# VectorE's order in a step of the second block's attention: masks of a step before its Fourier units

## The chip, the cores and the metric

One core of a Trainium2 chip runs the whole program. The metric is the device time of one execution in microseconds; the figure for the kernel before is the median of three runs.

## The reference

Two layers of a first block (four kinds of attention) are followed by two layers of a second block, on 512 tokens of width 1024 in fp32. What the change touches is the second block's mixing stage:

```python
def second_block(x, ...):
    for l in range(DEPTH):
        h = rmsnorm(x, norm1[l])
        p = h @ w_in[l]                       # u | q | k | v
        y_f = fourier_mix(u, w_fourier[l], b_fourier[l])
        q, k = rope(rmsnorm(q, q_norm[l])), rope(rmsnorm(k, k_norm[l]))
        y_a = windowed_gqa(q, k, v, sink[l])
        mix = jnp.concatenate([rmsnorm(y_f, g_fourier_out[l]), rmsnorm(y_a, g_attn_out[l])], axis=-1)
        x = x + mix @ w_o[l]
        ...                                   # gated feed-forward with a 3-tap convolution

def fourier_mix(u, w_f, b_f):
    f = jnp.fft.fft2(u.astype(jnp.float32), axes=(1, 2), norm="ortho").real.astype(u.dtype)
    return f @ w_f + b_f
```

`windowed_gqa` is attention of 8 heads on blocks of 128 queries; each query sees keys at a distance of at most 128, and a sink term enters the softmax.

## The kernel before

Every engine has one instruction stream, written out by hand, and semaphores between them. Large products are made of three fp32r matmuls each (`r3`, recorded at L494): both operands are split into a rounded high part (ScalarE's copy) and a low part (VectorE's or POOL's subtraction). Weights come in chunks through two slots: SP loads, ScalarE rounds (L974), POOL subtracts (L480).

In the second block, the attention of a layer is 16 steps, each for a pair of heads (`par` 0 and 1) and one block of 128 queries; `qt` counts 0 to 3, and a step has 256 score columns where `qt` is 0 or 3, 384 where it is 1 or 2. Beside it runs the Fourier work, cut into units: `units_in_step` gives two per step in this block. Eight units make the rest of the u projection (its last six tiles, the first two in halves), eight the product A with the sequence DFT, four the tiles Pj, four the tiles Qj, then two are empty and four make y. They fill steps 0 to 14.

TensorE's step t (L531): scores of t (L542), after the exponentials of t-1; where `(t - 2) % 4 == 3` a spread of the inverse row sums over the partitions (`spread_heads`, L580); the product of probabilities and values for t-2 (L556); the transposes of the probabilities of t-1 (L566); the two units of t.

ScalarE's step t (L1007): the two units of t-1 (rounding of u at L1230 and of A at L1250, copies of Pj, rounding of the Fourier result at L1261), then the two exponentials of t (L1019), at `qt` 3 two sink terms (L1025), and the square of a finished output pair (L1277).

VectorE's step t (L1419): the two units of t-1, then masks and maxima of t (`mask_and_max`, L1465, with a read of the accumulator), then the row sums where due (L1479, L1480) and the copies of the transposed probabilities of t-1 (L1438), then work on finished pairs (`take_pair`, L1763, and sums of squares, L1658). VectorE's units, in `fourier` (L1716), are: the low part of a u tile (`u_lo`, L1710), that of an A tile (L1729), nothing for Pj, for each Qj the combination of Pj and Qj (L1739, L1740) and the low part of the result before (`f_lo`, L1755), later the sums of the squares of y (L1658).

Outputs of TensorE go to PSUM banks by a plan computed beforehand (`ring_plan`, L123). In this stage units and the spreads take banks 0 and 1 in turn, transposes banks 2 and 3, and a bank is taken again when the engine that reads its tile last has freed it: for u and A tiles VectorE's low part, for Pj ScalarE's copy, for Qj VectorE's combination, for y ScalarE. The spread of step 5 takes the bank of the first A tile of step 4. Before the first A tile TensorE waits for all u tiles of the second half to be freed, before the first Pj for the last four A tiles, before the first y for all four low parts of the Fourier result.

Of the kernel before, what the change touches and what calls it, by code (L numbers as in the profile page):

```python
# [117 lines left out]
def units_in_step(block, t):  # L118

    return 3 if block == 1 and t < 6 else 2  # L120
# [112 lines left out]
def build(nc, dram, out):  # L233
# [3 lines left out]
    with ctx:  # L237
# [101 lines left out]
        def S(name):  # L339
            if name not in sems:  # L340
                sems[name] = ctx.enter_context(nc.semaphore(name))
            return sems[name]
# [20 lines left out]
        def bank(name):  # L363
            return banks[ring[name][1]]

        def wait_full(eng, name, i=None, per=0):

            v = ring[name][0] + 1
            eng.wait_ge(S("ring_full"), v if i is None else i * per + v)

        def freed(name):
            return S(f"ring_freed{ring[name][1]}")
# [8 lines left out]
        def per_row(tile, it):  # L381

            c = 4 * it["par"] + it["qt"]
            return tile[:, it["o"] % 2, c:c + 1]
# [26 lines left out]
        block = ctx.enter_context(nc.Block())  # L411
# [940 lines left out]
        def _(dve):  # L1352
# [66 lines left out]
            def attention(pairs, l, block, finish, between, scale_gate=None):  # L1419
                N = len(pairs)  # L1420
                for t in range(N + 5):
                    if t >= 1:
                        for _ in range(units_in_step(block, t - 1)):
                            next(between, None)
                    if t < N:
                        for it in pairs[t]:
                            dve.wait_ge(S("scores_ready"), it["n"] + 1)
                            mask_and_max(it, l).then_inc(S("max_ready"), 1)
                    if 1 <= t <= N:
                        pair = pairs[t - 1]  # L1430
                        if pair[0]["qt"] == TT - 1:
                            row_sums(pair)
                        for it in pair:
                            n, w = it["n"], it["nb"] * P
                            wait_full(dve, ("T", n))
                            if t >= 2:
                                dve.wait_ge(S("pv_done"), n - 1)
                            v.tensor_copy(probs_t[:, it["par"], 0:w], bank(("T", n))[:, 0:w]).then_inc(freed(("T", n)), 1)  # L1438
                    if scale_gate and t >= 2 and (t - 2) % TT == TT - 1:
                        scale_gate(pairs[t - 2][1])  # L1440
                    if t >= 3 and (t - 3) % TT == TT - 1:
                        finish(pairs[t - 3][1], 0)
                    if t >= 4 and (t - 4) % TT == TT - 1:
                        finish(pairs[t - 4][1], 1)
                for _ in between:
                    pass

            def mask_and_max(it, l):

                w, nb, b, h = it["nb"] * P, it["nb"], it["branch"], it["h"]  # L1450
                s, top = s_bank[it["par"]][:, 0:w], per_row(neg_max, it)
                blocks = s.rearrange("p (b c) -> p b c", c=P)
                m0 = it["k0"] - it["qt"] + 1
                if b == "M":
                    return v.tensor_reduce(top, s, AX.X, ALU.max, negate=True)  # L1455
                if b == "A":
                    return v.tensor_tensor_reduce(out=s, in0=s, in1=bias_r[:, h, w - 1::-1], scale=-1.0, scalar=BIG,  # L1457
                                                  op0=ALU.add, op1=ALU.min, accum_out=top)
                if b == "B":
                    return v.tensor_tensor_reduce(out=blocks[:, ::-1, :], in0=blocks[:, ::-1, :], in1=masks[:, 1:1 + nb, :], scale=-1.0,  # L1460
                                                  scalar=BIG, op0=ALU.add, op1=ALU.min, accum_out=top)
                if b == "C":
                    return v.tensor_tensor_reduce(out=blocks, in0=blocks, in1=masks[:, m0:m0 + nb, :], scale=-1.0,
                                                  scalar=neg_sink[:, l, h:h + 1], op0=ALU.add, op1=ALU.min, accum_out=top)
                return v.tensor_tensor_reduce(out=blocks, in0=blocks, in1=masks[:, 5 + m0:5 + m0 + nb, :],  # L1465
                                              scale=head_inv[:, it["pair"], it["qt"], it["par"]:it["par"] + 1],
                                              scalar=neg_sink[:, l, 4 + h:5 + h], op0=ALU.add, op1=ALU.min, accum_out=top)
# [3 lines left out]
            def row_sums(pair):  # L1471

                it = pair[1]
                sums = row_sum[:, it["o"] % 2, :]
                dve.wait_ge(S("exp_done"), it["n"] + 1)
                if it["sink"]:
                    sinks[0] += 2
                    dve.wait_ge(S("sink_exp"), sinks[0])
                    step(v.tensor_tensor(sums, sums, sink_exp[:, :], ALU.add))  # L1479
                v.reciprocal(row_inv[:, it["o"] % 2, :], sums).then_inc(S("inv_ready"), 1)  # L1480
# [27 lines left out]
            for l in range(DEPTH):  # L1508
# [63 lines left out]
                def scale_gate(it):  # L1572
                    n, tile, name = it["o"] % 8, it["tile"], ("bc", it["o"])
                    if n in (0, 2):
                        for t in range(2):
                            wait_taken(dve, ("w", l, f"{'am'[n // 2]}g{t}"))
                    if n == 4:
                        dve.wait_ge(S("gates_ready"), l + 1)
                        wait_taken(dve, ("w", l, "cg1"))
                    if n >= 6:  # L1580
                        wait_taken(dve, ("w", l, f"bg{n - 6}"))
                    wait_full(dve, name)
                    v.tensor_tensor(g[:, tile, :], bank(name)[:, :], g[:, tile, :], ALU.mult).then_inc(freed(name), 1)

                def gate_pair(it, part):
# [5 lines left out]
                    elif n == 7:  # L1591
                        out_lo(l, n)

                attention(PAIRS[l], l, 1, gate_pair, later_projections(), scale_gate)

                def centred_pair(k):
# [46 lines left out]
            for l in range(DEPTH):  # L1643
# [114 lines left out]
                def take_pair(it, part):  # L1758
# [5 lines left out]
                    elif k >= 1:  # L1764
                        sum_squares("ya", ya_squares, k)

                attention(PAIRS[DEPTH + l], l, 2, take_pair, fourier())
                wait_taken(dve, ("mix_ms", l))
                v.reciprocal(rtok[:, :], stat[:, :]).then_inc(S("mix_inv"), 1)
# [213 lines left out]
```

## Time and profile before

| | us |
|---|---|
| median of 3 runs | 1852.99 (1846.31 to 1853.43) |
| profiled execution | 1850.35 |
| its span | 1848.4 |
| TensorE busy (matmul) | 1750.2 |
| VectorE busy | 776.8 |
| ScalarE busy | 701.2 |
| POOL busy | 692.2 |

The profile records one execution: for each instruction its start, duration, line and engine (PE is TensorE, DVE VectorE, ACT ScalarE). Ends of matmuls are modelled, so durations in a row of matmuls overlap; starts are used below. In a timeline row "x4" means that four records were merged, and the duration then runs from the first start to the last end; what stands in brackets is the idle time of the engine before the instruction and what ended it. The windows give the busy time of each engine in a stretch and the clock that TensorE was granted, 1.00 being 2.4 GHz.

### The profile page before, as it was taken

What the parts mean: (1) busy time and instruction counts of PE and PEld (TensorE: products, weight loads), DVE (VectorE), ACT (ScalarE), POOL (GpSimd) and SP (SyncE); (2) the same over time, 40 slices, a digit from 0 to 9 for tenths busy, and PEclk for the clock granted to TensorE, in tenths of its full rate; (3) what the DMA queues carried; (4) which work ended last, traced back from release to release, by engine and by line L of the source; (5) the groups of instructions that cost most, each with busy time, mean ns of one, the idle gap of its engine ahead of it and who ended that gap; (6) DMA issues with size and microseconds to landing.
All of it is one profiled execution on the core that took longest, in us unless ns stands there. A gap on an engine that the chain in (4) does not pass through costs nothing.

```text
span 1848.4 us, 24688 instructions
## 1 busy us (share of the span) xinstructions
PE 1750.2 (95%) x9084; PEld 1379.2 (75%) x9084; DVE 776.8 (42%) x1470; ACT 701.2 (38%) x1136; POOL 692.2 (37%) x553
## 2 busy tenths in 40 slices
PE   6998999899899989989999999999997999999999
PEld 5775568787566767867788888877785878888887
DVE  7126464402655264554455115522455345502441
ACT  4444441524445053444343223433355334312331
POOL 3423116442310642325344344345231634434433
PEclk9999989899998979999999999999999999999999
DMA  6211103221110211112222223122211222232222
GB/s 254 92 69 47 47 24 118 89 91 70 47 47 24 103 40 53 70 47 69 91 91 79 101 98 107 67 98 88 70 50 44 91 91 91 74 108 92 102 74 95
DMA packets 24895, 148.02 MB, mean 80 GB/s; under 512 B 3184, under 2 KB 3568, under 8 KB 10736
## 3 DMA queue, kind: packets, MB, share of 16 engines
q1 hardware_dynamic: 22128, 140.13, 21.7%
q10 hardware_dynamic: 2688, 6.82, 1.0%
q8 instruction: 52, 0.85, 0.2%
q14 instruction: 27, 0.22, 0.0%
HBM read 144.84 MB, written 2.10 MB: 79 GB/s over the span
## 4 chain that ended last, share of the span: by engine, by line
PE 50%; issue 31%; POOL 11%; DVE 3%; ACT 3%; DMA 1%; POOLq 0%; ACTq 0%; DVEq 0%
PE ring L494 38%; POOL w_lo L480 11%; PE scores L542 3%; PE ring L566 2%; PE outs L556 2%; PE ring L580 1%; PE ring L637 1%; DMA xt<-in_x 1%; ACT probs L1019 1%; PE ring L874 1%; DVE g L1664 1%; PE ring L610 1%; ACT w_hi L974 1%; POOL w_hi L470 1%; DVE mix_l L1669 0%
## 5 line engine op out<-in xcount | busy, mean ns | idle before, releaser
L480 POOL TENSOR_TENSOR w_lo<-w_stage,w_hi 128x258 fp32r<-128x258 f32 (+5 forms) x517 | 670.7, 1330 | 1116.6 <-ACT w_hi L974 691.1
L494 PE MATMUL ring<-xh,w_lo 128*128 128x512 f32 x1296 | 522.3, 403 | 36.0 <-POOL w_lo L480 14.5
L494 PE MATMUL ring<-xh,w_hi 128*128 128x512 f32 x1296 | 515.4, 398 | 0.0
L494 PE MATMUL ring<-xl,w_hi 128*128 128x512 f32 x1296 | 515.1, 397 | 0.0
L494 PEld LDWEIGHTS ring<-xh,w_lo 128*128 128x128 f32 x1296 | 246.9, 191 | 100.3 <-issue 15.5
L494 PEld LDWEIGHTS ring<-xh,w_hi 128*128 128x128 f32 x1296 | 246.7, 190 | 56.5
L494 PEld LDWEIGHTS ring<-xl,w_hi 128*128 128x128 f32 x1296 | 247.3, 191 | 53.6
L1305 ACT ACTIVATE w_hi<-w_stage 128x2048 fp32r<-128x2048 f32 (+2 forms) x72 | 120.5, 1673 | 158.7 <-PE ring L494 158.7
L1315 ACT ACTIVATE g<-ring,convw 128x512 f32<-128x512 f32 x88 | 68.2, 779 | 261.3 <-DVE ring L1800 261.3
L974 ACT ACTIVATE w_hi<-w_stage 128x2064 fp32r<-128x2064 f32 (+2 forms) x77 | 123.0, 1607 | 88.2 <-PE ring L494 87.9
L1019 ACT ACTIVATE probs<-scores,neg_max 128x256 f32<-128x256 f32 (+2 forms) x192 | 96.1, 503 | 131.4 <-DVE neg_max L1455 28.2
L494 PE MATMUL ring<-act_l,w_hi 128*128 128x512 f32 x352 | 139.7, 397 | 0.0
L494 PE MATMUL ring<-act_h,w_lo 128*128 128x512 f32 x352 | 139.1, 395 | 0.0
L494 PE MATMUL ring<-act_h,w_hi 128*128 128x512 f32 x352 | 138.5, 394 | 0.0
L1800 DVE TENSOR_TENSOR ring<-ring,tmp 128x512 f32<-128x512 f32 x88 | 61.2, 699 | 183.0 <-PE ring L494 173.1
L1782 DVE TENSOR_TENSOR xt<-xt,ring 128x512 f32<-128x512 f32 x48 | 33.0, 687 | 248.2 <-PE ring L494 248.2
L1438 DVE COPY probs_t<-ring 128x256 f32<-128x256 f32 (+2 forms) x192 | 79.8, 455 | 35.8 <-PE ring L566 34.7
L494 PEld LDWEIGHTS ring<-act_h,w_lo 128*128 128x128 f32 x352 | 66.0, 188 | 17.2 <-DVE act_l L1813 0.7
L494 PEld LDWEIGHTS ring<-act_h,w_hi 128*128 128x128 f32 x352 | 66.0, 188 | 16.0
L494 PEld LDWEIGHTS ring<-act_l,w_hi 128*128 128x128 f32 x352 | 66.0, 188 | 15.6
L1457 DVE CUSTOM_DVE_ANT_0 scores<-scores,bias_r 128x128 f32<-128x128 f32 (+3 forms) x32 | 15.1, 514 | 135.9 <-PE scores L542 135.9
L566 PE MATMUL ring<-ident,probs 128*128 128x128 f32 x440 | 72.2, 294 | 0.0
(266 smaller groups left out, 2319.8 us busy)
## 6 DMA issues: line engine op xcount, KB each, us to landing
w_stage<-in_mixed SPq DMA_DIRECT2D x64, 1032.0 KB, 4.8
w_stage<-in_up SPq DMA_DIRECT2D x44, 1024.0 KB, 4.9
w_stage<-in_down SPq DMA_DIRECT2D x16, 768.0 KB, 4.3
w_stage<-in_down SPq DMA_DIRECT2D x16, 640.0 KB, 3.8
xt<-in_x ACTq DMA_DIRECT2D x4, 512.0 KB, 11.5
out_t<-xt ACTq DMA_DIRECT2D x8, 256.0 KB, 2.0
mem_f<-in_mem SPq DMA_DIRECT2D x1, 1024.0 KB, 9.8
bias_r<-in_relb SPq DMA_DIRECT2D x1, 1024.0 KB, 11.1
```

Of the source, the lines that this page charges most:

```text
L480: ins = nc.gpsimd.tensor_tensor(w_lo[:, slot, cols], w_stage[:, slot, cols], w_hi[:, slot, cols].bitcast(F32), ALU.subtract)
L494: ins = nc.tensor.matmul(o, lhs, rhs, start=start, stop=stop, skip_group_check=True)
L542: nc.tensor.matmul(s_bank[it["par"]][:, 0:it["nb"] * P], q_of(it), k_of(it, l), start=True, stop=True, skip_group_check=True).then_inc(S(" ...
L556: ins = nc.tensor.matmul(o_bank[it["o"] % 2][lo:lo + 64, it["qt"] * P:it["qt"] * P + P], v_of(it, l, j), probs_t[:, it["par"], j * P:j * P ...
L566: ins = nc.tensor.transpose(o[:, j * P:j * P + P], probs[:, it["n"] % 3, j * P:j * P + P], ident[:, :])
L974: ins = A(w_hi[:, c % 2, first:last], w_stage[:, c % 2, first:last], ACT.Copy)
L1019: A(probs[:, n % 3, 0:w], s_bank[it["par"]][:, 0:w], ACT.Exp, bias=per_row(neg_max, it), scale=1.0 if it["branch"] == "M" else -1.0, accum ...
L1305: A(w_hi[:, c % 2, 0:width], w_stage[:, c % 2, 0:width], ACT.Copy).then_inc(S("w_hi_done"), 1)
L1315: A(g[:, 4 * s + 2 + v, :], bank((kind, l, f0 + first + s))[:, :], ACT.Identity, bias=convw[:, l, taps, 4 * v + 3:4 * v + 4], scale=convw[ ...
L1438: v.tensor_copy(probs_t[:, it["par"], 0:w], bank(("T", n))[:, 0:w]).then_inc(freed(("T", n)), 1)
L1782: v.tensor_tensor(xt[:, k, :], xt[:, k, :], bank(name)[:, :], ALU.add).then_inc(freed(name), 1)
L1800: v.tensor_tensor(bank(name)[:, :], bank(name)[:, :], tmp[:, 0, :], ALU.mult).then_inc(S("normed"), 1)
```

## The change

In VectorE's attention loop the units of t-1 keep their place for block 1. For block 2 they are issued after the masks and maxima of step t instead of before them; they still come before the row sums and copies of the step. The instructions themselves, their number and their semaphores are the same, and so are the streams of the other engines.

```diff
--- before.py
+++ after.py
@@ -1419,13 +1419,16 @@
             def attention(pairs, l, block, finish, between, scale_gate=None):
                 N = len(pairs)
                 for t in range(N + 5):
-                    if t >= 1:
+                    if t >= 1 and block == 1:
                         for _ in range(units_in_step(block, t - 1)):
                             next(between, None)
                     if t < N:
                         for it in pairs[t]:
                             dve.wait_ge(S("scores_ready"), it["n"] + 1)
                             mask_and_max(it, l).then_inc(S("max_ready"), 1)
+                    if t >= 1 and block == 2:
+                        for _ in range(units_in_step(block, t - 1)):
+                            next(between, None)
                     if 1 <= t <= N:
                         pair = pairs[t - 1]
                         if pair[0]["qt"] == TT - 1:
```

## Rows read from the trace of the kernel before

**Rows 1.** The page's span, then windows of both stages: busy us (count) by engine, clock.

```profile
span 1848.4 us, 24688 instructions
...
725.00:822.00 97.00, 90.46 (x744) 74.93 (x746) 51.06 (x141) 48.47 (x115) 34.64 (x48) 0.98 0.19 67
1317.00:1413.00 96.00, 89.08 (x752) 74.03 (x752) 51.32 (x141) 49.41 (x116) 34.67 (x48) 1.00 0.20 67
```

**Rows 2.** Timeline, first layer, step 6: start, duration, instruction, idle before it.

```profile
759.89 0.92 PE L542 MATMUL scores<-k,q 64*128 64x384 f32 x4
...
760.84 0.69 DVE L1465 CUSTOM_DVE_ANT_0 scores<-scores,masks,neg_sink 128x384 f32<-128x384 f32 x1
...
761.96 0.36 PE L494 MATMUL ring<-w_hi,u_l 128*128 128x258 f32 x1
...
762.04 1.02 DVE L1438 COPY probs_t<-ring 128x384 f32<-128x384 f32 x2
```

**Rows 3.** Timeline, first layer, steps 4 and 5.

```profile
748.95 0.70 PE L542 MATMUL scores<-k,q 64*128 64x256 f32 x4
...
750.80 0.36 PE L494 MATMUL ring<-w_hi,u_l 128*128 128x258 f32 x1
...
754.15 0.92 PE L542 MATMUL scores<-k,q 64*128 64x384 f32 x4 [0.23 <-ACT probs L1019]
...
754.40 0.76 DVE L1729 TENSOR_TENSOR a_l<-ring,a_h 128x258 fp32r<-128x258 f32 x2 [2.35 <-ACT a_h L1250]
...
754.99 1.09 PE L580 MATMUL ring<-ident,row_inv 128*64 128x128 f32 x16
...
755.10 0.69 DVE L1465 CUSTOM_DVE_ANT_0 scores<-scores,masks,neg_sink 128x384 f32<-128x384 f32 x1
```

**Rows 4.** Timeline, first layer, step 11 to the start of step 13.

```profile
784.65 0.42 DVE L1739 TENSOR_TENSOR sq<-pj,ring 128x257 f32<-128x257 f32 x1
...
785.92 0.70 PE L542 MATMUL scores<-k,q 64*128 64x256 f32 x4
...
788.38 0.47 ACT L1019 ACTIVATE probs<-scores,neg_max 128x256 f32<-128x256 f32 x1 [0.80 <-DVE neg_max L1465]
...
790.33 1.31 DVE L1658 TENSOR_TENSOR tmp<-tmp 128x512 f32<-128x512 f32 x1 [0.65 <-ACT tmp L1277]
...
791.57 0.41 DVE L1739 TENSOR_TENSOR sq<-pj,ring 128x257 f32<-128x257 f32 x1
...
794.03 0.63 ACT L1261 ACTIVATE f_h<-sq 128x512 fp32r<-128x512 f32 x1 [1.00 <-DVEq L1742]
...
795.47 0.47 ACT L1019 ACTIVATE probs<-scores,neg_max 128x256 f32<-128x256 f32 x1 [0.81 <-DVE neg_max L1465]
...
796.56 1.65 PE L542 MATMUL scores<-k,q 64*128 64x384 f32 x4 [3.39 <-ACT probs L1019]
```

**Rows 5.** Timeline, first layer, step 15 to the last spread.

```profile
815.85 0.70 PE L542 MATMUL scores<-k,q 64*128 64x256 f32 x4
...
816.58 0.55 DVE L1465 CUSTOM_DVE_ANT_0 scores<-scores,masks,neg_sink 128x256 f32<-128x256 f32 x1 [1.35 <-PE scores L542]
...
817.05 0.55 DVE L1465 CUSTOM_DVE_ANT_0 scores<-scores,masks,neg_sink 128x256 f32<-128x256 f32 x1
...
817.87 1.02 DVE L1438 COPY probs_t<-ring 128x384 f32<-128x384 f32 x2 [0.21 <-PE ring L566]
...
819.04 0.88 PE L556 MATMUL outs<-probs_t,v 128*64 128x128 f32 x12 [0.88 <-DVE probs_t L1438]
...
819.42 0.69 DVE L1658 TENSOR_TENSOR tmp<-tmp 128x512 f32<-128x512 f32 x1 [0.53 <-ACT tmp L1277]
...
821.08 1.09 PE L580 MATMUL ring<-ident,row_inv 128*64 128x128 f32 x16 [0.58 <-DVE row_inv L1480]
```

**Rows 6.** Windows from the scores of step 13, first and second layer, as in rows 1.

```profile
796.60:799.60 3.00, 3.00 (x18) 1.92 (x20) 2.04 (x6) 0.00 (x0) 0.00 (x0) 0.50 0.03 5
1388.60:1391.60 3.00, 2.91 (x33) 2.19 (x34) 2.40 (x7) 0.04 (x1) 0.00 (x0) 1.00 0.04 11
```

## The prediction

> **What bounds the kernel now.** I read the span and the windows of the two second-block attention stages first, because only these stages are touched [rows 1]. TensorE is busy 90.5 of 97 us in the first layer and 89.1 of 96 in the second, at full clock but for one stretch, while VectorE works 51 us. So TensorE's instruction stream sets the end, and a stage gets longer by exactly the time that TensorE newly waits, shorter only by a wait that it loses. 6.5 and 6.9 us of waits are there to be lost, in all. Then I read the timelines of single steps, always from the start of the scores of step t, which I write S(t), and asked two things: how late TensorE needs something that VectorE gives, and how late VectorE gives it once the pair of masks stands in front.
>
> In one step TensorE issues scores(t), at steps 5, 9, 13 the spread of the inverse sums, the probabilities-times-values of t-2, the transposes of t-1, then two units of Fourier work. VectorE, before, did the two units of t-1, masks of t, copies of t-1. The first unit's low part was mostly done while TensorE still worked on the second unit, the second one's in the gap between S(t) and the moment at which the masks could start. The masks could not start much earlier: on an idle VectorE they start 0.73 us after S(t) with 256 columns [rows 5], and in step 6, with the low part just finished, 0.95 us after S(t) with 384 columns [rows 2]. Step 5 has the same 0.95 [rows 3], though its low parts ended elsewhere, so I take it for the floor of a wide step; nothing is then gained there, and in a narrow step 0.1 to 0.3 us that nobody waits for. Were the floor 0.73 in wide steps too, (a) and (b) below would each be 0.2 less.
>
> **The change part by part.** No instruction is added or removed, no DMA is moved; POOL's and SP's queues see only later releases. What moves is a pair of masks ahead of two units. A pair holds VectorE 1.20 us at 384 columns (760.84 to 762.04, [rows 2]) and 0.93 at 256 (twice 816.58 to 817.05, [rows 5]). The new wait for scores(t) now stands in front of the units of t-1, so these are queued behind S(t) + 2.15 us (384) or S(t) + 1.66 us (256). Who waits for them is TensorE, through the two ring banks 0 and 1 that all units share.
>
> (a) Steps 3 to 8, the unit's bank. In step 6 the first unit needs the bank of the first A tile of step 5. It starts at S + 2.07 (759.89 to 761.96, [rows 2]); the low part will be done at 0.95 + 1.20 + 0.43 = 2.58, 0.43 us being one low part, of which two take 0.76 [rows 3]. Stall 0.5. In step 4 the first A tile needs all u tiles split, thus both low parts: 0.73 + 0.93 + 0.76 = 2.42, against 1.85 (748.95 to 750.80, [rows 3]): stall 0.6. Step 8 has the same pattern (the P tiles need both last A tiles): 0.6. Steps 3 and 7 need one low part at 0.73 + 0.93 + 0.43 = 2.09, against the 2.07 of the six-transpose pattern: 0. Steps 1 and 2 need nothing of the step itself. Together 1.7.
>
> (b) Step 5. The spread of the inverse sums comes right behind the scores, and its bank is that of the first A tile of step 4. Before, the two low parts ran at 754.40, before the spread at 754.99, S + 0.84 [rows 3]. The mask already started at 755.10, S + 0.95, so it gains nothing, and the bank comes free at 0.95 + 1.20 + 0.4 = 2.55. Stall 1.7. At steps 9 and 13 the spread's bank is not waited for: its last holders are a P tile, freed by ScalarE, and the third Q tile, freed a step before.
>
> (c) Steps 11 to 13, the Fourier pairs. I call ft the pair of VectorE instructions that combines a P and a Q tile. ScalarE rounds two ft results before it takes the exponentials of the step, and this order is unchanged. Before, ft(0) ran at 784.65, ahead of S(11) = 785.92. Now it starts at 785.92 + 1.66 = 787.58; ft(1) follows after some 0.85 (two instructions of 0.42 [rows 4]), ScalarE can round it at 789.3 and reach its exponentials at 789.9, not at 788.38: 1.5 later. (TensorE's third Q tile would meanwhile wait 0.4 for its bank; this is inside the sum below, not added.) The square that ScalarE makes behind them, and VectorE's sum of it, which began at 790.33, come at 791.85. That sum took 1.31 us while POOL was splitting weights, against 0.69 of the same line later [rows 4, 5]; so it ends at 792.5 to 793.1 instead of 791.57, and the masks of step 12 start there, since S(12) is past. From that point the old path to the exponentials was 795.47 - 791.57 = 3.90; the new one is 0.93 of masks, 2.46 to the second rounding (791.57 to 794.03), and 0.6 of rounding: 3.99. So scores(13), which already waited 3.39 us for these exponentials [rows 4], start 1.0 to 1.6 later. I take 1.3. The masks are off this chain in name only: what ends last is the exponential behind two roundings, and they now wait for the masks.
>
> The Trainium skill (GPSIMD Engine Reference, Specifications) says that GpSimd shares its SBUF interfaces with VectorE and collides with VectorE instructions that have two SBUF inputs. The 1.31 against 0.69 us agrees with that; one pair of rows is little, and POOL may be done by then, so I let the price be open between the two.
>
> (d) Steps 15 to 17. Two sums of y squares were done before the masks of step 15, in idle time; now they stand between masks and copies. The masks end at 817.51; two sums at 0.62 follow; the copies that began at 817.87 begin at 818.75, and TensorE's product, which already waited for them until 819.04, starts 0.9 later. What ends last is VectorE's chain: the sum at 819.42 moves to some 819.8, and the last spread at 821.08 by the same 0.4 [rows 5]. Price 0.4, and 0.9 if the chain doesn't catch up.
>
> Step 13's own rest (the last low part behind the masks) is hidden: it ends at S(13) + 0.95 + 1.20 + 0.7 = 2.85, and before the y tiles TensorE has the spread (at 0.84, for 1.09 [rows 3]) and some 1.0 of product and transposes (1.15 with six transposes, [rows 2]), together 2.9; at most 0.1.
>
> **Sum.** 1.7 + 1.7 + 1.3 + 0.4 = 5.1 us per layer. The second layer repeats the pattern to some hundredths, so 10.2 in all. Behind the stage come projections bound by TensorE that hide nothing. The profiled execution took 1850.35 us (span 1848.4 and 1.95 around it), 2.64 below the median of 1852.99; the sum gives 1860.6 against the one and 1863.2 against the other. I take 1862. Bounds per layer: (a) 0.8 to 2.2 (each stall 0.2 us less or 0.1 more), (b) 1.4 to 1.9, (c) 0.9 to 1.7, (d) 0.2 to 0.9; no part can be a gain of more than 0.1, as nothing that TensorE waits for comes sooner. 3.3 to 6.7, thus 6.6 to 13.4 in all.
>
> **Rivals.** First, the other sign: the early masks bring the exponentials of step 12 forward and shorten TensorE's wait of 3.39 us at S(13). If ScalarE met its exponentials first, masks (0.93) and one low part (0.7) would leave that chain: 1.6 per layer, 1847; it decides as soon as the banks of (a) and (b) turn out free in time. Against it speaks ScalarE's order, with both roundings ahead. 7 in 100, with everything from 1846 to 1852.
>
> Second, the clock. After the 3.39 us wait of the first layer the granted clock was 0.50 over 3 us, the 1.2 GHz level, and the scores took 1.65 us; in the second layer, after an equal wait, it stayed at 1.00 [rows 4, 6]. At half clock 3 us of work cost 1.5 more. New idle of 1.7 us in step 5 and a longer one at S(13) could bring one to three such stretches: 1.5 to 4.5 us, 1863.5 to 1866.5. That layer kept full clock through all its waits, 6.9 us of them [rows 1]. 22 in 100. The Trainium skill (TensorE: Matmul & The Clock Gate, HAM oscillation) warns that idling between groups of matmuls brings the low clock back again and again; the first layer agrees, the second doesn't. By it alone each layer would lose once more, 1865.
>
> Third, only the chains cost: the bank stalls of (a) and (b) are mostly absorbed, because the profile's ends are modelled and low parts release earlier than I read. Then (c) + (d) remain, 1.7 per layer: 1855.5. 14 in 100.
>
> **How the numbers follow.** The forecast, 1858 to 1865 about 1862, has 57 in 100. The range 1855 to 1868 leaves out the first rival and the far end of the second. Half a per cent, about what a measurement of this kernel can tell from no change, is 9.3 us: 1862.3 against the median. The forecast's sum lies little above it, so it gives two thirds of its weight to slower; the second rival nearly all; the third none. Slower 0.60, same 0.37, faster 0.03.
>
> **What would show it.** In the changed profile: TensorE's L580 of step 5 starts 2.5 us after its scores, with a wait of 1.7 put to the low part at L1729, in both layers; first units of steps 4 and 8 at S + 2.4 and of step 6 at S + 2.6; masks at S + 0.95 or S + 0.73 in every step, no sooner; the wait of scores(13) for L1019 at 4 us or more; the copies of step 15 about 1.2 us after its masks end. Both stages longer by 5, all others as before. I am wrong if L580 of step 5 still starts at S + 0.84, if the exponentials of step 12 come less than 3.9 us after S(12), or if the granted clock falls in step 5.

## The result and the profile after

| | before | after |
|---|---|---|
| median of the runs, us | 1851.49 (1846.31 to 1853.43, 4 runs) | 1867.37 (1864.29 to 1871.61, 4 runs) |
| profiled execution, its span | 1850.35, 1848.4 | 1864.29, 1862.5 |
| TensorE busy | 1750.2 | 1757.9 |
| VectorE busy | 776.8 | 774.6 |

The ratio of the runs is 1.0092, 95% interval 1.0061 to 1.0123: the changed kernel is 11 to 23 us slower, some 16 by the medians. The forecast of 1862 had the sign and the places; it had about 9 to 10 us where 16 to 17 came. Carried over to the 1852.99 us that the prediction started from, the ratio gives 1870, beyond the upper end of its range, 1868.

In the changed kernel the lines of VectorE's code move by three: the masks are at L1468, the low parts of u and A at L1713 and L1732, the combination at L1742 and L1743, `f_lo` at L1758, the copies at L1441, the sums of squares at L1661.

**Steps 4, 5 and 6** (answers to [rows 2, 3]). Timeline of the changed kernel, first layer; the columns are start, duration, instruction, and idle time before it with what ended it.

```profile
749.57 0.70 PE L542 MATMUL scores<-k,q 64*128 64x256 f32 x4
...
751.24 0.87 DVE L1713 SCALAR_TENSOR_TENSOR u_l<-ring,rtok,u_h 128x256 fp32r<-128x256 f32 x2
...
752.37 0.36 PE L494 MATMUL ring<-w_hi,u_l 128*128 128x258 f32 x1 [0.70 <-DVE u_l L1713]
...
755.71 0.92 PE L542 MATMUL scores<-k,q 64*128 64x384 f32 x4 [0.23 <-ACT probs L1019]
...
756.66 0.69 DVE L1468 CUSTOM_DVE_ANT_0 scores<-scores,masks,neg_sink 128x384 f32<-128x384 f32 x1 [3.47 <-PE scores L542]
...
757.86 0.76 DVE L1732 TENSOR_TENSOR a_l<-ring,a_h 128x258 fp32r<-128x258 f32 x2
...
758.43 1.09 PE L580 MATMUL ring<-ident,row_inv 128*64 128x128 f32 x16 [1.80 <-DVE a_l L1732]
...
763.35 0.92 PE L542 MATMUL scores<-k,q 64*128 64x384 f32 x4
...
765.97 0.39 PE L494 MATMUL ring<-w_hi,u_l 128*128 128x258 f32 x1 [0.32 <-DVE a_l L1732]
```

The mask of step 5 starts 0.95 us after the scores, as before. VectorE had been idle 3.47 us by then, and through the last of it two A tiles, rounded by 756.20, waited for their low parts. The low parts follow at 757.86, and the spread, which came 0.84 us after the scores, now comes 2.72 after them. The A tile of step 4 comes 2.80 us after its scores instead of 1.85, the unit of step 6 2.62 instead of 2.07. In step 8 (scores at 774.26) the first P tile waits for two low parts of A, which end at 776.68 (the view shows 0.75 us for the pair), and comes 2.78 us after its scores:

```profile
775.93 0.75 DVE L1732 TENSOR_TENSOR a_l<-ring,a_h 128x258 fp32r<-128x258 f32 x2
...
777.04 0.36 PE L494 MATMUL ring<-a_h,w_lo 128*128 128x258 f32 x1 [0.69 <-DVE a_l L1732]
```

**Step 11 to the start of step 13** (answers to [rows 4]), same kernel and layer.

```profile
791.00 0.70 PE L542 MATMUL scores<-k,q 64*128 64x256 f32 x4
...
792.67 0.42 DVE L1742 TENSOR_TENSOR sq<-pj,ring 128x257 f32<-128x257 f32 x1
...
794.55 0.98 DVE L1758 TENSOR_TENSOR f_l<-sq,f_h 128x512 fp32r<-128x512 f32 x1 [0.16 <-DVE sq L1743]
...
795.02 0.46 ACT L1019 ACTIVATE probs<-scores,neg_max 128x256 f32<-128x256 f32 x1
...
796.95 0.69 DVE L1661 TENSOR_TENSOR tmp<-tmp 128x512 f32<-128x512 f32 x1 [0.36 <-ACT tmp L1277]
...
797.56 0.55 DVE L1468 CUSTOM_DVE_ANT_0 scores<-scores,masks,neg_sink 128x256 f32<-128x256 f32 x1
...
801.50 0.46 ACT L1019 ACTIVATE probs<-scores,neg_max 128x256 f32<-128x256 f32 x1
802.55 1.65 PE L542 MATMUL scores<-k,q 64*128 64x384 f32 x4 [3.95 <-ACT probs L1019]
```

From the masks of step 12 to its exponentials are 3.94 us; the old path was 3.90. Scores(13) start 11.55 after scores(11), before it was 10.64.

**The end of the stage** (answers to [rows 5]).

```profile
822.43 0.70 PE L542 MATMUL scores<-k,q 64*128 64x256 f32 x4
...
823.17 0.55 DVE L1468 CUSTOM_DVE_ANT_0 scores<-scores,masks,neg_sink 128x256 f32<-128x256 f32 x1 [4.81 <-PE scores L542]
...
825.50 1.01 DVE L1441 COPY probs_t<-ring 128x384 f32<-128x384 f32 x2
...
826.66 0.88 PE L556 MATMUL outs<-probs_t,v 128*64 128x128 f32 x12 [1.92 <-DVE probs_t L1441]
...
828.37 1.98 PE L580 MATMUL ring<-ident,row_inv 128*64 128x128 f32 x16
```

Two sums of squares now stand between masks and copies; TensorE's product waits 1.92 us instead of 0.88. And the spread takes 1.98 us instead of 1.09, at half clock.

**The clock** (answers to [rows 1, 6]). Windows of the changed kernel: the numbers at the end of a line are granted clock, DMA share and GB/s.

```profile
725.00:841.00 116.00, 101.31 (x786) 83.47 (x787) 55.62 (x150) 54.12 (x123) 34.10 (x48) 0.93 0.16 56
1322.00:1438.00 116.00, 101.37 (x788) 83.44 (x789) 55.63 (x151) 54.65 (x123) 34.07 (x48) 0.94 0.16 56
...
828.00:831.00 3.00, 3.00 (x27) 2.46 (x25) 0.88 (x3) 0.60 (x1) 0.00 (x0) 0.50 0.00 0
834.00:845.00 11.00, 9.26 (x33) 7.54 (x33) 7.97 (x14) 4.67 (x8) 0.00 (x0) 0.53 0.00 0
1397.00:1405.00 8.00, 5.78 (x35) 4.29 (x36) 4.78 (x14) 1.55 (x6) 0.00 (x0) 0.57 0.10 42
```

The same 116 us of the kernel before, from its own start of the stage:

```profile
725.00:841.00 116.00, 104.90 (x815) 85.69 (x816) 63.51 (x161) 58.70 (x130) 36.44 (x51) 0.97 0.16 56
1317.00:1433.00 116.00, 104.55 (x821) 85.61 (x822) 63.77 (x161) 60.06 (x130) 37.90 (x53) 0.99 0.16 56
```

At a clock of 0.93 and 0.94 instead of 0.97 and 0.99 the changed kernel spent about 30 us of the two stretches at the 1.2 GHz level, before about 10. The 3.4 us behind scores(13) in one layer have become some 7 in both (0.57 over the 8 us from 1397 is 6.9 us at half clock), and the 3.4 us behind the last spreads of each layer have become two pieces, in the first layer one of them some 10 us long.

**Length of each step**, from the starts of its scores to those of the next, worked out from the timelines (us):

| from the scores of step | before, 1st layer | after | before, 2nd layer | after |
|---|---|---|---|---|
| 3 | 7.94 | 8.10 | 7.70 | 7.86 |
| 4 | 5.20 | 6.14 | 5.21 | 6.13 |
| 5 | 5.74 | 7.64 | 5.76 | 7.64 |
| 6 | 5.11 | 5.71 | 5.14 | 5.72 |
| 7 | 5.12 | 5.20 | 5.12 | 5.23 |
| 8 | 4.90 | 5.84 | 4.90 | 5.82 |
| 9, 10 together | 10.90 | 10.90 | 10.89 | 10.89 |
| 11 | 5.15 | 5.51 | 5.13 | 5.55 |
| 12 | 5.49 | 6.04 | 5.52 | 6.01 |
| 13 | 11.45 | 12.04 | 9.87 | 12.34 |
| 14 | 7.84 | 7.84 | 7.82 | 7.82 |
| 15 to the last spread L580 | 5.23 | 5.94 | 5.24 | 5.66 |
| on to the spread L619 | 5.55 | 6.75 | 5.55 | 6.75 |
| on to the output projection | 4.46 | 4.93 | 4.48 | 4.92 |

The rows "on to" are TensorE's work behind the last step: it spreads the inverse norms (L619) and begins the output projection. From scores(0) to the output projection the two layers take 114.27 and 114.00 us instead of 105.75 and 103.98, 18.5 us more. The span grew by 14.1 only: outside the stages the profiled execution of before had more half clock than that of after (of the shift, 3 us came back in front of the second layer's attention and 1 us in each feed-forward), which no experiment here addresses. The timed runs had 16.

### The profile page after: what moved, and what is told of

Read it like the earlier page. It is cut to its first block, busy times and chain, and to the rows that moved or that the text cites. A ratio compares the mean times of both kernels' runs of the same rounds, so it can differ in the third digit from the quotient of the medians.

```text
span 1862.5 us, 24682 instructions
## 1 busy us (share of the span) xinstructions
PE 1757.9 (94%) x9084; PEld 1385.4 (74%) x9084; DVE 774.6 (42%) x1470; ACT 701.2 (38%) x1136; POOL 690.7 (37%) x553
## 4 chain that ended last, share of the span: by engine, by line
PE 49%; issue 31%; POOL 11%; DVE 4%; ACT 3%; DMA 1%; POOLq 0%; ACTq 0%; DVEq 0%
PE ring L494 38%; POOL w_lo L480 11%; PE scores L542 3%; PE ring L566 2%; PE outs L556 2%; PE ring L580 1%; PE ring L637 1%; ACT probs L1019 1%; DMA xt<-in_x 1%; PE ring L874 1%; DVE scores L1468 1%; DVE g L1667 1%; PE ring L610 1%; ACT w_hi L974 1%; POOL w_hi L470 1%
## 5 line engine op out<-in xcount | busy, mean ns | idle before, releaser
L1441 DVE COPY probs_t<-ring 128x256 f32<-128x256 f32 (+2 forms) x192 | 80.1, 456 | 38.3 <-PE ring L566 37.2
L494 PEld LDWEIGHTS ring<-act_l,w_hi 128*128 128x128 f32 x352 | 66.0, 188 | 15.6
L1468 DVE CUSTOM_DVE_ANT_0 scores<-scores,masks,neg_sink 128x256 f32<-128x256 f32 (+1 forms) x64 | 36.8, 617 | 97.0 <-PE scores L542 97.0
```

Of the source, the lines that this page charges most:

```text
L494: ins = nc.tensor.matmul(o, lhs, rhs, start=start, stop=stop, skip_group_check=True)
```

## The experiments

Ratios and differences are against the kernel before, run on the same chip and at the same time as the experiment. The changed kernel was timed apart from them, so a comparison of an experiment with it goes over two measurements.

**Step 5 alone.** VectorE's order of the change, for one step of sixteen:

```diff
-                    if t >= 1:
+                    late = t >= 1 and block == 2 and (t == 5)
+                    if t >= 1 and not late:
                         for _ in range(units_in_step(block, t - 1)):
                             next(between, None)
                     ...                                    # masks and maxima of t
+                    if late:
+                        for _ in range(units_in_step(block, t - 1)):
+                            next(between, None)
```

> Masks first in step 5 of the second block alone. My theory (the banks 0 and 1 that units and spreads share): the spread of step 5 starts 2.7 us after its scores instead of 0.84, with a wait of 1.8 put to the low part of A, in both layers; every other step keeps its length; +1.9 us a layer, +3.8 in all, the clock rows as before. If instead the change costs by its chains in steps 11 to 17 alone (rival), this kernel takes the time of before, within 1 us.

Measured: 1.0032 (1.0018 to 1.0047), 1854.31 against 1849.10 us. Step 5 takes 7.62 us instead of 5.74 in the first layer, every other step up to the twelfth keeps its length, and the wait is put to the low part. Timeline of this kernel in the second layer:

```profile
1349.87 0.92 PE L542 MATMUL scores<-k,q 64*128 64x384 f32 x4 [0.23 <-ACT probs L1019]
1352.58 1.48 PE L580 MATMUL ring<-ident,row_inv 128*64 128x128 f32 x16 [1.80 <-DVE a_l L1733]
1353.78 1.13 PE L556 MATMUL outs<-probs_t,v 128*64 128x128 f32 x8
```

The window right behind it, read as those above:

```profile
1355.00:1357.00 2.00, 2.00 (x12) 2.00 (x13) 0.85 (x2) 1.16 (x3) 0.00 (x0) 0.61 0.62 153
```

The wait is the same 1.80 us, but here the clock fell right behind it, and step 5 took 9.21 instead of 5.76. In the first layer it did not fall. So the bank's wait is shown. A second cost beside it, which the expectation had left out, shows in one layer of the trace, and this execution (1861.03 us) was the second slowest of the kernel's twelve. The times alone don't show it: 3.8 us were expected, some 6 came, and the interval reaches from 3.3 to 8.7.

**Steps 1 to 10 alone** (the condition is `t <= 10`).

> Masks first in steps 1 to 10 alone. Theory: steps 3 to 8 grow by 0.2, 0.9, 1.9, 0.6, 0.1 and 0.9 us as in the changed kernel, 4.6 a layer and 9.2 in all; the wait at scores(13) stays 3.4 us and the low clock behind it as before. If the low clock of the changed kernel comes from the many new waits of steps 3 to 8, it shows here too, with another 2 to 5 us.

Measured: 1.0065 (1.0049 to 1.0080), 12 us. The steps have the lengths of the changed kernel to 0.05 us (steps 4 to 8 of the first layer: 6.14, 7.64, 5.70, 5.22, 5.85), 4.6 us a layer, and steps 11 and 12 those of before. The 9.2 us of stalls lie just inside the interval (9.1 to 14.8). In the trace step 13 takes 11.50 us in both layers where the second layer of before had 9.87, behind an unchanged wait; but with the old order it took 11.26 to 12.28 in the other layers too (first layer of the kernel before, both layers with step 5 alone and with steps 15 and 16 alone), so this is no cost of the change. The way from the last spread to the next is 5.55 us in both layers, as before. Where the other 3 us are, if they are real, is open.

**From step 11 on alone** (`t >= 11`).

> Masks first from step 11 on alone. Theory: steps 11 and 12 grow by 0.4 and 0.5 us, the end of the stage by 0.5: 1.4 a layer, 2.8 in all, and on top what a longer wait at scores(13) (3.9 instead of 3.4 us) brings in half clock, 0 to 2.5 us a layer. If half clock belongs to steps 3 to 8, the sum stays at 2.8.

Measured: 1.0035 (1.0016 to 1.0054), 6.5 us. Steps 11 and 12 take 5.54 and 6.02 in the first layer, 5.56 and 5.99 in the second; from scores(15) to the last spread 5.66 and 5.90. That is the 1.4 us a layer. The trace shows half clock beside it: step 13 at 12.55 and 11.45, the way to the next spread at 6.13 and 6.76 instead of 5.55. The interval is 3.0 to 10 us, so that the 2.8 of stalls is just outside it. The longer way to the next spread, which steps 1 to 10 alone don't have, belongs to this half of the change. The two ratios add to 1.0100, the whole change had 1.0092.

**The masks between the two units.**

```diff
-                    if t >= 1:
-                        for _ in range(units_in_step(block, t - 1)):
-                            next(between, None)
+                    units = units_in_step(block, t - 1) if t >= 1 else 0
+                    for _ in range(units if block == 1 else min(units, 1)):
+                        next(between, None)
                     ...                                    # masks and maxima of t
+                    for _ in range(0 if block == 1 else units - 1):
+                        next(between, None)
```

> The masks of a step come between its two Fourier units: the first unit's low part ahead of them, the second's behind. Theory: whoever waits for the first unit only (the spread of step 5, the first unit of steps 3, 6, 7 and the third Q tile) waits no more; steps 4 and 8, where TensorE needs both, keep 0.5 to 0.7 us each, and one postponed result remains in the chains of steps 11 to 17: 1.2 us a layer in steps 3 to 8, against 4.6 of the changed kernel; 2.5 to 5 us in all above before. If what costs is that the masks hold VectorE at all, and not which bank is behind them, the time is that of the changed kernel, +14.

Measured: 1.0020 (1.0005 to 1.0035), 3.7 us where 2.5 to 5 were expected. Timeline of this kernel, steps 4 and 5 of the first layer:

```profile
751.46 0.36 PE L494 MATMUL ring<-w_hi,u_l 128*128 128x258 f32 x1 [0.31 <-DVE u_l L1712]
...
755.06 0.43 DVE L1731 TENSOR_TENSOR a_l<-ring,a_h 128x258 fp32r<-128x258 f32 x1 [2.78 <-ACT a_h L1250]
755.65 1.09 PE L580 MATMUL ring<-ident,row_inv 128*64 128x128 f32 x16
755.75 0.69 DVE L1467 CUSTOM_DVE_ANT_0 scores<-scores,masks,neg_sink 128x384 f32<-128x384 f32 x1 [0.27 <-PE scores L542]
```

With the first low part ahead of the masks, the spread is back at 0.85 us after its scores (754.80), steps 3, 5, 6, 7 and 11 have their old lengths, and only steps 4 and 8, where TensorE needs both low parts, keep 0.54 and 0.61. The masks start when they did. What costs is which bank stands behind the masks, not the time that they hold VectorE.

**The changed kernel, with work in TensorE's wait.** At the end of step 12 TensorE multiplies the identity by itself into the bank that the next spread overwrites; the results are used by nothing.

```diff
                     for _ in range(units_in_step(block, t)):
                         next(between, None)
+                    if block == 2 and t == 12:
+                        name = ("bc", pairs[11][0]["o"])
+                        pe.wait_ge(freed(name), ring[name][2])
+                        for _ in range(22):
+                            nc.tensor.matmul(bank(name)[:, 0:P], ident[:, :], ident[:, :], start=True, stop=True, skip_group_check=True)
```

> The changed kernel, with 22 more matmuls (identity by identity, 128 columns, into the ring bank that the next spread will overwrite) at the end of TensorE's step 12, so that TensorE works in most of its wait at scores(13). They take about 2.3 us of a wait of 3.9 and delay nothing. Theory: if half clock follows from that wait, steps 13 to 14 take 9.9 us in both layers instead of 12.0 and 12.3, and the kernel gains 2 to 5 us on the changed one (1863 to 1865 beside 1867). If the clock falls by a phase of its own, the length of step 13 is unchanged or random and the time that of the changed kernel.

Measured: 1864.39 us, 1.0076 (1.0058 to 1.0094). My size was off: one such matmul takes 0.235 us, 22 take 5.2 and not 2.3, so scores(13) came 1.8 us late.

```profile
798.89 5.18 PE L574 MATMUL ring<-ident 128*128 128x128 f32 x44 [0.66 <-DVE sq L1748]
804.00 0.92 PE L542 MATMUL scores<-k,q 64*128 64x384 f32 x4
```

But the scores took 0.92 us and not 1.65, and step 13 took 10.09 us in both layers, where the changed kernel had 12.04 and 12.34.

**The kernel before with 26 of them.**

> The kernel before with 26 such matmuls in the wait of 3.4 us at scores(13). Theory: half clock behind this wait disappears where it came (step 13 at 9.9 us instead of 11.5 in the first layer); 0 to 3 us less than before. Rival (a phase of its own): no change.

Measured: 1.0020 (1.0008 to 1.0032). Too long again: step 12 took 7.83 instead of 5.5 us. Step 13 took 9.88 in both layers. Inconclusive as a time; both fillings were repeated with 12.

**The changed kernel with 12.**

> The changed kernel with 12 matmuls in its wait at scores(13) instead of 22: one takes 0.235 us, 12 some 2.8 us of the 3.2 in which their bank is free, so that step 12 keeps its 6.0 us. Theory (a wait costs its length and then half clock): step 13 at 9.9 to 10.1 us in both layers instead of 12.0 and 12.3, 4 us less than the changed kernel, about 1863, and 12 to 13 us above before, which is the sum of the stalls alone. If the clock is no part of the cost, no difference from the changed kernel, 17 above before.

Measured: 1862.67 us, 1.0059 (1.0043 to 1.0075), 12.0 us above before.

```profile
801.94 2.94 PE L574 MATMUL ring<-ident 128*128 128x128 f32 x24 [0.65 <-DVE sq L1748]
...
805.21 0.92 PE L542 MATMUL scores<-k,q 64*128 64x384 f32 x4 [0.32 <-ACT probs L1024]
```

Scores(13) come where they came, with 0.32 us of wait left instead of 3.95, and step 13 takes 10.08 and 10.09 us. This kernel computes the same and does more, and is 4.7 us below the changed kernel's median; the intervals of the two ratios overlap, so this difference by itself is not shown. The expected 1863 and 12 to 13 us came; the way to the spread L619 stayed at 6.75 in both layers, so half clock at the end of the stage is still in it.

**The kernel before with 12.**

> The kernel before with 12 such matmuls. Theory: step 12 keeps 5.5 us, step 13 takes 9.9 in both layers; 1 to 3 us less than the kernel before in the mean, as it has half clock there in at least one layer. Rival: no difference.

Measured: 0.9978 (0.9966 to 0.9989), 3.6 us faster than before. Step 12 keeps 5.49 and 5.51, step 13 takes 9.88 in both layers.

```profile
796.33 0.92 PE L542 MATMUL scores<-k,q 64*128 64x384 f32 x4 [0.72 <-ACT probs L1024]
```

This kernel and the one before it were timed together, and they differ by nothing but the change: 1862.67 against 1847.04 us, 15.6 us, with full clock in step 13 of both layers of both. That is about what the change cost without the matmuls. The matmuls take 3.6 us from the order of before and 4.7 from the changed one, nearly the same: half clock behind scores(13) is paid in both orders.

**Low parts behind the masks, everything else ahead.** In steps 11 and 12 of the kernel before, only the last `f_lo` of the step goes behind the masks.

```diff
                     ...                                    # masks and maxima of t
+                    while postponed:
+                        low_part[0](postponed.pop(0))
                     ...                                    # in the units of the Qj
-                        if j >= 1:
-                            f_lo(j - 1)
+                        if j == 2:
+                            f_lo(1)
+                        if j % 2 == 1:
+                            postponed.append(j - 1)
                         yield
```

> The kernel before, its units ahead of the masks, but in steps 11 and 12 the last low part (L1755) goes behind the masks of the step: the chain to the exponentials loses it, and nothing is put into it. Theory of the chain (steps 11 to 13: what ends last is the exponential behind masks and roundings): masks of step 11 start 0.7 us sooner and those of step 12 1.4 us sooner, scores(13) wait 2.0 us instead of 3.4; 2.8 us less in both layers, and perhaps 1.5 to 3 us more if the clock stays up. If ScalarE's order sets the wait alone, nothing changes.

Measured: 1.0004 (0.9992 to 1.0017), no difference. The chain did what was expected in size:

```profile
789.03 1.08 DVE L1761 TENSOR_TENSOR f_l<-sq,f_h 128x512 fp32r<-128x512 f32 x1
...
796.51 0.92 PE L542 MATMUL scores<-k,q 64*128 64x384 f32 x4 [2.31 <-ACT probs L1019]
```

Step 12 takes 4.40 and 4.42 us instead of 5.5, 1.1 us less in each layer (1.4 expected; a low part beside POOL took 1.08 us here, not 0.69). The clock took it back in the profiled execution: step 13 is 11.49 and 12.55 us, the way from the last spread on 6.36 and 5.79.

**The same with 10 matmuls in the wait.**

> The one before this, with 10 matmuls more in the wait of 2 us at scores(13). Theory: as before this, with full clock in step 13 of both layers for certain: 3 to 6 us less than the kernel before.

Measured: 0.9976 (0.9965 to 0.9988), 3.3 us faster than before. Step 12 keeps 4.4 us and step 13 takes 9.87 in both layers. Timed together with the kernel above, from which it differs by the 10 matmuls alone, it takes 1846.44 us against 1851.09.

**Steps 15 and 16 alone** (`t in (15, 16)`).

> Masks first in steps 15 and 16 alone. My prediction had 0.4 us a layer. Theory from the trace of the changed kernel: from scores(15) to the last spread 5.7 us instead of 5.2, 0.9 in all; and if the longer wait before the product of step 16 (1.9 instead of 0.9 us) brings half clock, the way from the last spread to the next takes 6.4 to 6.8 instead of 5.6 us, 1 to 2.5 us in all more.

Measured: 1.0013 (1.0001 to 1.0025), 2.4 us. In the second layer from scores(15) to the last spread 5.65 us; in the first 6.49, with half clock already in it, and then 6.84 and 6.25 instead of 5.55 to the next spread. Both parts came as expected, though the interval (0.2 to 4.6 us) would also hold the stalls alone.

**Full clock to the end of the stage.** The kernel with postponed low parts and 10 matmuls, with 5 more of them between the stage's last two sums of squares on TensorE (L610) and 2 before the spreads of the inverse norms (L619).

> The fastest so far (low parts postponed, 10 matmuls in the wait at scores(13)) with 7 more matmuls in TensorE's two waits between the last sums of squares and the spreads. Theory: full clock there too, 0.5 to 1.5 us a layer less, 4 to 6 us less than the kernel before. If the clock falls anyway, the same as without them.

Measured: 1844.24 us, 0.9966 (0.9956 to 0.9976), 6.4 us faster than before and 23 below the changed kernel. Its windows of both stages:

```profile
724.00:840.00 116.00, 108.82 (x860) 89.57 (x861) 63.94 (x161) 59.79 (x130) 39.05 (x55) 1.00 0.17 56
1313.00:1429.00 116.00, 109.63 (x861) 90.41 (x862) 63.93 (x161) 60.18 (x130) 39.27 (x55) 0.99 0.17 56
```

The stages take 102.72 and 102.44 us; the 0.99 comes from a piece behind the start of the output projection. It beats both kernels, and keeps the order of before where the change would have moved it. How much of the gain is due to the 7 matmuls at the end is open: the interval overlaps that of the kernel without them (0.9965 to 0.9988).

## Why the prediction was right or wrong

**What bounds it: right.** The stages got longer by what TensorE newly waits. Nothing was gained anywhere. The masks start 0.95 or 0.73 us after their scores (1.05 in step 12, 1.69 in step 13), the floor that I had read; this is 0.3 us sooner than before in steps 3 and 4, and 1.1 and 2.7 us sooner in steps 11 and 12, but no step got shorter by it, and the exponentials of step 12, for which TensorE waits, came 0.9 later.

**(a) The unit's bank: right in place, too small.** Predicted 1.7 us a layer, measured 2.7 (steps 3, 4, 6, 7, 8: 0.16, 0.94, 0.60, 0.08, 0.94 in the first layer). I took two low parts for 0.76 us, which is the pair of A; the pair of u takes 0.87. And I let TensorE start the moment a low part ended. In the changed kernel the low parts of step 4 end at 752.11 and the A tile starts at 752.37, 0.26 us later; those of step 8 end at 776.68, and the P tile starts at 777.04, 0.36 later. In step 6 it was 0.05. In the kernel before these waits did not end last, so no row of it showed the price; the bounds should have carried up to 0.4 for each. The mechanism held, but this term was too small, and "each stall 0.1 more" did not cover it. (Its lower bound, 0.8, doesn't follow from its own rule either: three stalls, each 0.2 less, give 1.1.)

**(b) The spread of step 5: right.** 1.9 us against 1.7, inside its bounds, with 0.15 us from the end of the low part to the spread; shown alone by the first experiment, and its absence by the masks between the units.

**(c) The chain to scores(13): right, the size was 0.9, not 1.3.** The square and its sum came 1.54 us later, as worked out (1.5). The sum took 0.69 and not 1.31 us, the lower of the two ends that I had left open, and the slower instruction was now `f_lo`, at 0.98. What made them slow shows in the traces of the two kernels: of the instructions of L1755 (L1758) and L1658 (L1661) in both layers, all that no POOL instruction overlapped took 0.68 or 0.69 us, while those that started during a POOL subtraction, or together with one, took 0.98 to 1.32. The `f_lo` at 787.00 in the kernel before, which started just ahead of a POOL subtraction, took 0.69, and POOL's took 1.21 us instead of 0.74. The rule of the Trainium skill quoted in the prediction (GPSIMD Engine Reference, Specifications) agrees with these times; no run took POOL away, so the cause itself is not shown. The low part of step 13 cost 0.2 us and not the 0.1 at most: step 13 takes 10.08 at full clock against 9.88.

**(d) The end of the stage: right.** 0.42 us in the second layer against 0.4.

**The sum of the stalls** is then 2.7 + 1.9 + 0.9 + 0.2 + 0.4 = 6.1 us a layer, 12.2 in all, where the prediction had 10.2 and bounds of 6.6 to 13.4. That the changed kernel with 12 matmuls came out 12.0 above before is no proof of this sum: that kernel before still pays its half clock at scores(13), and against the one with the same 12 matmuls the difference is 15.6.

**The clock: the step that failed.** I treated it as a rival, an event with 22 in 100 that would replace the forecast, and left it out of the sum. It is a term of the sum. In the profiled executions the two stages grew by 18.5 us, 12.2 of them stalls and 6.3 half clock; in the timed runs 4 of 16 are beyond the stalls. These 4 are known loosely, as the interval of 11 to 23 us would hold the stalls alone; the two kernels with 12 matmuls, timed together and closer, give 15.6.

I had argued that the second layer kept full clock through all its 6.9 us of waits. That was one profiled execution, and not even it was at full clock in the spreads behind the stage: its window, extended to 1433, reads 0.99. And it was the exception. With nothing in the wait, step 13 took 11.26 us or more, which means half clock, in 15 of the 16 layers profiled, after waits of 2.3 to 3.9 us; the one at full clock (9.87) is this one. In the old order of steps 11 and 12 alone it was seven layers of eight. With 10 to 26 matmuls in the wait step 13 took 9.87 to 10.09 in all twelve layers of six kernels. So the growth that the profiles show at scores(13) is for the most part a half clock that the kernel before has too, in nearly every execution, and the profile happened to miss.

What the change adds in half clock shows at the end of the stage. The way from the last spread L580 to the spread L619 took 5.55 to 6.37 us, 5.8 in the mean, in the fourteen layers of seven kernels with the old order there, and 5.64 to 6.84, 6.5 in the mean, in the ten layers of five kernels with the new one. That is 1.4 us in both layers; the last spread itself has some too (5.94 against 5.66 for the changed kernel's first layer). Behind the new wait of 1.80 us in step 5 the clock fell in one layer of ten. Where the other 2 us or so arise is open. With 4 us more in the sum the prediction would have read about 1866.

The Trainium skill (TensorE: Matmul & The Clock Gate, HAM oscillation) warned that a TensorE that idles between groups of matmuls loses the high clock again and again. I cited it and then weighed it against a single layer. The 15 layers of 16 agree with it.

**The rivals.** The first, an earlier exponential, is out: masks ahead of both units lengthened the way to it, and masks between the units left step 12 as it was (5.46 and 5.49 us). Its mechanism is real in another order, though: with only the low part behind the masks step 12 is 1.1 us shorter. The third, bank stalls absorbed, is refuted by steps 1 to 10 alone. The second is true, in addition to the forecast and not in its place; and as far as it could be placed, its place is the end of the stage, not step 5 or scores(13).

**Still open** is when exactly a wait of a given length costs the clock, where about half of the 4 us beyond the stalls arises, and why half clock outside the stages differed between profiled executions by several us.

## What to carry to other kernels

An engine that takes results for several consumers should not put a wait for the next stage in front of results that are already there: read, for each buffer that the moved work frees, how long after the new wait it comes free, and how long after the same point its next user starts, and add up to 0.4 us for handing over. Then count each microsecond that TensorE newly idles as more than one, since some of these waits are followed by half clock, and don't take from one profiled execution whether a given wait is: here the one layer that kept its clock was one in sixteen. Where a wait can't be removed, a few matmuls without use that fit inside it can be worth more than the reordering: 12 of them gained 3.6 us here on the kernel before.

## What the runs showed of the hardware

- After the same wait the granted clock fell or did not: after 1.80 us in step 5 in one layer of ten (9.21 against 7.62 us for the step), after 3.4 us before scores(13) in seven of eight (11.45 against 9.87), after 2.3 us there in both layers of the one kernel that had it (11.49 and 12.55).
- Matmuls of the identity with itself (128x128, fp32) kept the clock up through such a wait, in twelve layers of twelve; one takes 0.235 us and leaves two records in the trace.
- From the end of a low part on VectorE to TensorE's first instruction that waited for it passed 0.26 us in step 4, 0.15 in step 5, 0.05 in step 6 and 0.36 in step 8.
- A VectorE subtraction or sum of 128x512 elements took 0.69 us, and 0.98 to 1.32 when it started during a POOL subtraction or together with one; some of the POOL subtractions during which VectorE's ran took about 1.2 us instead of 0.74.
- Half clock showed in the length of TensorE's instructions: 1.65 instead of 0.92 us for the four score matmuls, 1.98 instead of 1.09 for the sixteen of a spread.
